# Side-by-side start of a fused two-layer trunk over pieces of weights and activations

## The reference, cut to what matters

```python
h = rms_norm(r, norm_mix_pre[layer])
proj = h @ w_in[layer]          # q latent 384 | kv latent 256 | rope key 32 | dq | dk | dv | gates
# latent attention and differential attention, gated, projected
r = r + rms_norm(mix, norm_mix_post[layer])
h = rms_norm(r, norm_ffn_pre[layer])
r = r + rms_norm((silu(gate) * up) @ w_down[layer], norm_ffn_post[layer])
```

## Time and profile before

| | us |
|---|---|
| median of 3 runs (lowest to highest) | 840.55 (839.25 to 840.62) |
| the profiled execution, its own time | 839.78 |
| its span in the trace | 837.8 |
| PE busy in the span | 820.7 |
| DVE busy in the span | 611.0 |
| ACT busy in the span | 460.1 |
| POOL busy in the span | 127.5 |

### The profile page before, as it was taken

How to read it: one execution, slowest core, us unless ns; L and a number is a source line. 1 busy time by engine, 2 the same in 40 slices (tenths; PEclk the granted TensorE clock), 3 DMA queues, 4 the chain that set the end, 5 groups by cost and what they waited for, 6 DMA issues and landing times.

```text
span 837.8 us, 17756 instructions
## 1 busy us (share of the span) xinstructions
PE 820.7 (98%) x6711; PEld 805.3 (96%) x6711; DVE 611.0 (73%) x1015; ACT 460.1 (55%) x754; POOL 127.5 (15%) x131
## 2 busy tenths in 40 slices
PE   8999999999999999999999999999999999999995
PEld 8998999999999999999999999899999999999995
DVE  5899586569597666666668995866787877667763
ACT  6656555474565444455556556555665744545550
POOL 2112000004331111101112220000143111111010
PEclk9999999999999999999999999999999999999998
DMA  8666423225536555356653665233462665644631
GB/s 289 217 186 203 146 77 101 80 98 190 163 101 217 184 158 186 116 153 183 188 173 107 196 200 178 76 102 101 147 208 75 224 197 182 193 145 150 192 124 51
DMA packets 40554, 131.05 MB, mean 156 GB/s; under 512 B 4528, under 2 KB 5936, under 8 KB 40496
## 3 DMA queue, kind: packets, MB, share of 16 engines
q1 hardware_dynamic: 40496, 130.24, 48.8%
HBM read 129.18 MB, written 1.05 MB: 155 GB/s over the span
## 4 chain that ended last, share of the span: by engine, by line
PE 80%; DVE 14%; ACT 2%; issue 2%; DMA 1%; POOL 0%; SPq 0%; DVEq 0%; POOLq 0%
PE bank L1059 23%; PE bank L1061 22%; PE bank L1060 22%; DVE w_lo L660 4%; PE bank L1089 2%; PE bank L1284 2%; PE bank L1260 2%; PE bank L1108 1%; DVE h_lo L682 1%; PE bank L1299 1%; PE bank L1093 1%; DVE resid L697 1%; DVE tres L690 1%; DVE lat_lo L781 1%; ACT e_t L450 1%
## 5 line engine op out<-in xcount | busy, mean ns | idle before, releaser
L660 DVE TENSOR_TENSOR w_lo<-w_raw,w_hi 128x1024 fp32r<-128x1024 f32 x260 | 347.8, 1344 | 21.7 <-ACT w_hi L321 19.5
L1059 PE MATMUL bank<-h_hi,w_hi 128*128 128x272 f32 (+1 forms) x1232 | 358.3, 291 | 1.9 <-DVE lat L678 0.7
L1061 PE MATMUL bank<-h_hi,w_lo 128*128 128x272 f32 (+1 forms) x1232 | 352.8, 286 | 0.0
L1060 PE MATMUL bank<-h_lo,w_hi 128*128 128x272 f32 (+1 forms) x1232 | 351.8, 286 | 0.0
L321 ACT ACTIVATE w_hi<-w_raw 128x1024 fp32r<-128x1024 f32 x260 | 273.0, 1054 | 117.4 <-PE bank L1061 67.8
L1059 PEld LDWEIGHTS bank<-h_hi,w_hi 128*128 128x128 f32 x1232 | 232.6, 189 | 4.1 <-issue 2.2
L1061 PEld LDWEIGHTS bank<-h_hi,w_lo 128*128 128x128 f32 x1232 | 232.4, 189 | 0.0
L1060 PEld LDWEIGHTS bank<-h_lo,w_hi 128*128 128x128 f32 x1232 | 232.2, 188 | 0.0
L1061 PE MATMUL bank<-ff_hi,w_lo 128*128 128x272 f32 (+1 forms) x352 | 100.0, 284 | 0.0
L1059 PE MATMUL bank<-ff_hi,w_hi 128*128 128x272 f32 (+1 forms) x352 | 99.9, 284 | 0.0
L1060 PE MATMUL bank<-ff_lo,w_hi 128*128 128x272 f32 (+1 forms) x352 | 99.7, 283 | 0.0
(11 more groups left out here) (195 smaller groups left out, 1101.0 us busy)
## 6 DMA issues: line engine op xcount, KB each, us to landing
w_raw<-weights SPq DMA_DIRECT2D x198, 512.0 KB, 3.8
w_raw<-weights SPq DMA_DIRECT2D x32, 384.0 KB, 3.1
w_raw<-weights SPq DMA_DIRECT2D x32, 320.0 KB, 2.8
resid<-x_t SPq DMA_DIRECT2D x4, 272.0 KB, 4.7
out_t<-resid SPq DMA_DIRECT2D x4, 256.0 KB, 2.1
cst<-consts SPq DMA_DIRECT2D x1, 544.0 KB, 5.7
y<-consts SPq DMA_DIRECT2D x1, 256.0 KB, 4.9
b_t<-lam SPq DMA_DIRECT2D x1, 256.0 KB, 5.7
```

The source lines that it names most:

```text
L660: dve.tensor_tensor(w_lo[:, n % RING, :], w_raw[:, n % RAW, :], w_hi[:, n % RING, :].bitcast(f32), ALU.subtract).then_inc(lo_ready, 1)
L1059: pe.matmul(dst, wh, hi, start=first, stop=False)
L1060: pe.matmul(dst, wh, lo, start=False, stop=False)
L1061: return pe.matmul(dst, wl, hi, start=False, stop=last)
```

## The change

The first four slots get an input array of their own, in which each piece is contiguous for each partition, and a buffer of their own (`w_first`, over memory that is used later). The pieces are chunks 0, 1, 2-3, 4-5 and 6-7 of all four slots at once. The activations come in the same pieces; the gains travel in front of the first. Tiles 0 to 3 run side by side, one chunk after another: the high products of a piece first, then those with the low part of the activations, then those with the low part of the weights. Tiles 4 and 5 use banks 4 and 5 and wait for no bank. The norm's sums move from behind tile 2 to behind the first chunk of tile 4, its spread from chunk 6 of tile 3 to chunk 6 of tile 4. The loads of slots 4 to 7 wait for nothing. ScalarE splits slot 6 before the last square instead of after the root. VectorE splits slot 7 at tile 2 together with slot 8, and nothing at tile 1. `keep_clock(50)` becomes `keep_clock(34)`.

```diff
+GAIN_COLS = 80
+FIRST = 4
+PIECES = [(0, 1), (1, 2), (2, 4), (4, 6), (6, 8)]
...
+        (w_first,), _ = place(att0, [("w_first", [P, FIRST * SLOT], f32)])
...
+        def piece_of(w, a, b):
+            return w[:, FIRST * P * a:FIRST * P * b].rearrange("p (s c) -> p s c", s=FIRST)
+        def bank_of(t):
+            return t if t < FIRST + 2 else t % BANKS
...
-                if n >= RAW:
+                if n >= FIRST + RAW:
...
-            sp.dma_start(gain[:, :, :], gains.rearrange("p (l g) -> p l g", l=DEPTH)).then_inc(gain_in, 16)
-            two = weights[0:2 * P, :].rearrange("(s p) c -> p s c", s=2)
-            for q in range(4):
-                sp.dma_start(r[:, 2 * q:2 * q + 2, :], xc[:, 2 * q:2 * q + 2, :]).then_inc(x_in[q], 16)
-                if q in (0, 2):
-                    at = q * SLOT // 4
-                    sp.dma_start(w_raw[:, 0:2, at:at + SLOT // 2], two[:, :, at:at + SLOT // 2]).then_inc(half_in[q // 2], 16)
+            for q, (a, b) in enumerate(PIECES):
+                xs = slice(GAIN_COLS + a * TOK if q else 0, GAIN_COLS + b * TOK)
+                ws = slice(FIRST * P * a, FIRST * P * b)
+                sp.dma_start(x_sb[:, xs], xT[:, xs]).then_inc(x_in[q], 16)
+                sp.dma_start(w_first[:, ws], first_weights[:, ws]).then_inc(piece_in[q], 16)
             sp.dma_start(cst[:, 0:P], consts[:, 0:P]).then_inc(id_in, 16)
-            load(2, SLOT)
-            load(3, SLOT)
             load(4, SLOT)
+            load(5, SLOT)
             sp.dma_start(cst[:, P:], consts[:, 512:C_ALL]).then_inc(tables_in, 16)
-            load(5, SLOT)
+            load(6, SLOT)
+            load(7, SLOT)
...
-            first_hi(0, 1)
-            quarter_split(0)
-            quarter_split(1)
-            first_hi(2, 3)
-            first_squares(0, 1)
-            first_hi(4, 5)
-            quarter_split(2)
-            quarter_split(3)
-            first_hi(6, 7)
-            first_squares(2)
-            split(2)
-            first_squares(3, 4, 5, 6, 7)
-            for n in range(3, AHEAD):
-                split(n)
+            for q in range(len(PIECES)):
+                first_hi(q)
+                piece_split(q)
+                if q >= 2:
+                    first_squares(q - 2)
+            split(FIRST)
+            first_squares(3, 4)
+            split(FIRST + 1)
+            first_squares(5, 6)
+            split(FIRST + 2)
+            first_squares(7)
...
-                if l == 0:
-                    split(AHEAD)
...
+            for q, (a, b) in enumerate(PIECES):
+                dve.wait_ge(x_in[q], 16)
+                for c in range(a, b):
+                    lo_part(0, c, G_MIXPRE, 0, 0)
+                piece_split(q)
+            split(FIRST)
+            split(FIRST + 1)
...
-                    if i or not l:
-                        split(S("lat") + i + AHEAD)
+                    if l or i != 1:
+                        if l == 0 and i == 2:
+                            split(S("lat") + 1 + AHEAD)
+                        if i or not l:
+                            split(S("lat") + i + AHEAD)
...
+            def start_tiles(src):
+                for q, (a, b) in enumerate(PIECES):
+                    for k in range(a, b):
+                        pe.wait_ge(h_hi, k + 1)
...
+                        for t in range(FIRST):
+                            pe.matmul(ps[t][:, :TOK], w_hi[:, t, k * P:(k + 1) * P], src[k][0], start=k == 0, stop=False)
+                    for k in range(a, b):
+                        pe.wait_ge(h_lo, k + 1)
+                        for t in range(FIRST):
+                            pe.matmul(ps[t][:, :TOK], w_hi[:, t, k * P:(k + 1) * P], src[k][1], start=False, stop=False)
...
+                    for k in range(a, b):
+                        for t in range(FIRST):
+                            mm = pe.matmul(ps[t][:, :TOK], w_lo[:, t, k * P:(k + 1) * P], src[k][0], start=False, stop=k == KC - 1)
...
-            keep_clock(50)
+            keep_clock(34)
...
-                    first_tiles([(TL("lat") + q, S("lat") + q, late, t0) for q in range(2)], (h_hi, h_lo, 0),
...
-                    slot_ready(S("lat") + 2)
-                    tile(TL("lat") + 2, S("lat") + 2, 0, P, late, t0)
-                    norm_sums(K0 + PRE_MIX, 7, 0)
-                    pe.wait_ge(id_in, 16)
-                    slot_ready(S("lat") + 3)
-                    tile(TL("lat") + 3, S("lat") + 3, 0, P, full, 0, inside={6: lambda: norm_spread(K0 + PRE_MIX, 7, 0)})
+                    start_tiles(full)
...
+                    tile(TL("lat") + i, S("lat") + i, 0, P if i < 5 else HW, full, 0,
+                         inside={1: lambda: norm_sums(PRE_MIX, 7, 0), 6: first_spread} if (l, i) == (0, 4) else None)
```

More of the change, by code:

```diff
@@ L137, in __init__, with build_trunk @@
                     s += CHUNKS[k]
-def build_trunk(nc: bass.Bass, xT, weights, gains, lam_in, consts, outT):
+def build_trunk(nc: bass.Bass, xT, first_weights, weights, lam_in, consts, outT):
     f32, f32r, bf16 = mybir.dt.float32, mybir.dt.float32r, mybir.dt.bfloat16
@@ L354, in _, with first_hi, piece_split @@
             act.activation(idle_act, eps, ACT.Sqrt)
[L355 to L359, removed]
+            def first_hi(q):
+                act.wait_ge(x_in[q], 16)
+                for c in range(*PIECES[q]):
                     act.activation(hh[:, c, :], r[:, c, :], ACT.Copy, scale=gain[:, 0, G_MIXPRE + c:G_MIXPRE + c + 1]).then_inc(h_hi, 1)
[L362 to L366, removed]
+            def piece_split(q):
+                act.wait_ge(piece_in[q], 16)
+                a, b = PIECES[q]
+                ins = act.activation(w_hi[:, 0:FIRST, a * P:b * P], piece_of(w_first, a, b), ACT.Copy)
+                if b == KC:
+                    ins.then_inc(hi_ready, FIRST)
+                else:
+                    ins.then_inc(piece_hi, 1)
             def first_squares(*chunks):
@@ L677, in evac @@
                 dve.wait_ge(pe_done, plan.tile_done[t])
-                dve.tensor_tensor(dst, ps[t % BANKS][rows, t0:TOK], factor, ALU.mult).then_inc(tile_free, 1)
+                dve.tensor_tensor(dst, ps[bank_of(t)][rows, t0:TOK], factor, ALU.mult).then_inc(tile_free, 1)
             def lo_part(b, c, g, l, t0):
@@ L707, in _, with piece_split @@
             dve.memset(identb[:, :], 0.0).then_inc(warm_ready, 1)
[L708 to L725 removed]
+            dve.wait_ge(x_in[0], 16)
+            def piece_split(q):
+                a, b = PIECES[q]
+                if b == KC:
+                    dve.wait_ge(hi_ready, FIRST)
+                else:
+                    dve.wait_ge(piece_hi, q + 1)
+                ins = dve.tensor_tensor(w_lo[:, 0:FIRST, a * P:b * P], piece_of(w_first, a, b), w_hi[:, 0:FIRST, a * P:b * P].bitcast(f32), ALU.subtract)
+                if b == KC:
+                    ins.then_inc(lo_ready, FIRST)
+                else:
+                    ins.then_inc(piece_lo, 1)
+            for q, (a, b) in enumerate(PIECES):
[5 more added lines that the diff above has]
+            split(FIRST + 1)
             recip(PRE_MIX, 0)
@@ L1172, in _, with first_spread @@
                     slot_ready(S("lat") + i)
-                    tile(TL("lat") + i, S("lat") + i, 0, P if i < 5 else HW, full, 0)
+                    def first_spread():
+                        pe.wait_ge(id_in, 16)
+                        norm_spread(PRE_MIX, 7, 0)
+                    tile(TL("lat") + i, S("lat") + i, 0, P if i < 5 else HW, full, 0,
+                         inside={1: lambda: norm_sums(PRE_MIX, 7, 0), 6: first_spread} if (l, i) == (0, 4) else None)
                 def latent_spreads():
@@ L1487 @@
     gains = np.concatenate(cols, axis=1).transpose(2, 0, 1).reshape(P, DEPTH * GAINS)
+    x_t = np.concatenate([gains, np.zeros((P, GAIN_COLS - DEPTH * GAINS), np.float32), x_t], axis=1)
     lam = np.broadcast_to(A(diff_lambda).reshape(1, DEPTH * 4 * DIFF_DH), (P, DEPTH * 4 * DIFF_DH))
     packed = pack_weights(A(w_in), A(mla_w_uq), A(mla_w_ukv), A(w_o_mla), A(w_o_diff), A(w_out), A(w_gate_up), A(w_down))
-    arrays = {"x_t": x_t, "weights": packed, "gains": gains, "lam": lam, "consts": constants()}
+    first = packed[0:FIRST * P].reshape(FIRST, P, SLOT)
+    first = np.concatenate([first[:, :, a * P:b * P].transpose(1, 0, 2).reshape(P, -1) for a, b in PIECES], axis=1)
+    arrays = {"x_t": x_t, "first_weights": first, "weights": packed, "lam": lam, "consts": constants()}
     arrays = {k: np.ascontiguousarray(v) for k, v in arrays.items()}
```

58 lines of the change are left out of this document (26 added, 32 removed).

## The result

The changed kernel takes 844.89 us in the median of four runs (843.3 to 846.38), against 840.36 for the kernel before (839.25 to 840.62): a ratio of 1.0061, 95% interval 1.0048 to 1.0074 (the two medians alone give 1.0054, inside it). It is slower by 4.5 us by these medians, and 2.8 us above the dearest case that I had priced (842.1). The profiled execution took 844.19, with a span of 842.2, which is 4.4 us more than before.

The account below looks back on a forecast made before the run. VectorE was taken to bound the kernel up to 65 us. Taking the norm's factor 1.3 us sooner, less 0.6 lost at tile 1, gives 0.7: 840.55 - 0.7 = 839.8 us, range 837.9 to 841.5.

Parts of the forecast that it names:

- the dearest case: Clock falls behind the sums inside tile 4 and again at tile 9: 842.1 us.
- VectorE binds from the take to 65 us: From VectorE taking the norm's factor up to 65 us, the schedule hangs on VectorE, not PE.
- the take: VectorE taking the norm's factor, which starts its unbroken work; forecast at 22.3 against 23.64 us, 1.3 us sooner.
- PE starts at 5.0: First weights land at 4.4 us, ScalarE's copy takes 0.58, so PE's real work starts 2.45 us sooner.
- VectorE loses some time at tile 1: With its split moved behind tile 2, VectorE stands about 0.6 us at tile 1, bounds 0 and 0.7.
- PE's lead: PE gains 3.0 + 1.3 us of lead and spends it idle before tiles 6 to 9, mostly ahead of tile 9.
- the sum for the norm: Tile 4's first chunk to 18.4, norm sums to 19.9, five chunks 1.9, spread 0.5: VectorE takes the factor at 22.3 us.
- Chunks 2-3: In the side-by-side tiles, this piece lands at 7.9 us at 338 GB/s, is copied by 8.9; PE waits 0.9 us.
- My slower rival: Clock falls behind the sums inside tile 4: 15 matmuls x 0.10 us, 0.8 us slower, 841.3 us; chance 0.10.
- The line that I drew for the clock: Tile 4's 1.5 us low stretch lies between 1.40 us, where the clock held, and 1.85, where it fell.
- the change gains once all is in time: Factor taken 1.3 us sooner less 0.6 us lost at tile 1 gives 0.7 us net gain at tile 9's start.
- The fit that the prediction took: A transfer costs about 2.0 us fixed plus bytes at 436 GB/s; first weights land near 4.2, PE starts near 4.8.

Follow-up runs that it names:

- early squares: Changed kernel with ScalarE squaring pieces 0 to 2 right behind their high parts and pieces 3 and 4 behind their copies; 841.28 us.
- the other layout: Changed kernel with the first weights stored piece by piece in HBM, rows 2 or 4 KB apart instead of 16; 844.32 us.
- The filled kernel: Changed kernel with 28 warm-up matmuls ahead of the norm sums inside tile 4, in PE's wait for GpSimd's adds; 843.96 us.
- With pairs: Changed kernel with chunks 0 and 1 in one piece, so two chunks per piece throughout, and 50 warm-up matmuls; 842.77 us.
- the split back at tile 1: Changed kernel with VectorE's split put back at tile 1, slot i + 6 at every tile; 843.95 us.
- layout and squares mended: Changed kernel with the first weights stored piece by piece and ScalarE squaring each early piece as soon as it has it; 840.55 us.
- two of its variants: Changed kernel with ScalarE's squares made earlier, 841.28 us, and changed kernel with 28 warm-up matmuls ahead of tile 4's norm sums, 843.96 us.

## Why the prediction was wrong

**Right.** That VectorE binds from the take to 65 us and that the first emptying, which follows the take, decides: the table says so, and between 28 and 72 us VectorE nowhere waits for PE in the changed kernel. That PE starts at 5.0 (4.90; in another execution, with early squares, the first piece came late and it was 6.45). That VectorE loses some time at tile 1 (0.59 us of standing, 0.45 net). That PE's lead is spent waiting ahead of tiles 6 to 9 (3.7 us in three waits, 2.41 of them ahead of tile 9). That root and reciprocal lie beside the five chunks: they run at 23.39 and 23.68, the spread at 26.62.

**The step that failed** is the sum for the norm: "PE does the first chunk of tile 4 to 18.4, the first six sums (0.7 of 1.4 for twelve, rows 3), waits shortly for the last square, ends at 19.9". I asked when the last square would be there and never laid out GpSimd's adds, which stand between each square and the next but one; their chain stood in the sum at nothing. I looked for the bound at the load of slot 6 (its split was over at 20.6 in the profile, and the last square waited for GpSimd, not for it). The terms, in the profile:

- The four tiles and the first chunk ended at 20.2, not 18.4: 1.8 us. Chunks 2-3 began at 10.56, not 8.9; I had 338 GB/s in the start, and it was 208 and 238. This lateness alone would not have set the time: with the other layout PE was there sooner and waited 1.94 instead of 1.65 us for the adds.
- The last add ended at 21.8, so sums from 21.85 to 23.2, which is 3.0 us behind the first chunk and not the 1.5 of my sum: another 1.5 us. The chain of adds begins only at 12.9, since ScalarE squares behind the copies of pieces that come late, and two of its adds take twice their time beside VectorE's subtractions. Early squares alone give back 3.6 us.
- The clock fell behind the sums: 15 x 0.10 = 1.5 us. The filled kernel and the one with early squares show that it holds there when the stretch of waiting and sums is 1.3 us. My slower rival had the place and the price of this fall, and no term for the late adds.

Together 4.8 of the 4.9 us by which the take was missed.

The line that I drew for the clock, held behind 1.40 us and fallen behind 1.85, does not hold up either. With pairs it held behind 2.7 us of waiting and sums, while with the split back at tile 1 it fell after 1.8 us of them and 1.5 us of products. The length of such a stretch alone does not say whether the clock falls, so both my chance for the slower rival and this part of the loss rest on something that the runs do not settle.

Also wrong is that the change gains once all is in time: with layout and squares mended the time is 840.55 against 839.82 (1.0001 to 1.0019), 0.7 us slower instead of faster. The take was then only 0.48 us sooner than before, and the way from the first emptying to tile 9 was 0.44 us longer (16.65 against 16.21); the 0.3 us behind tile 9 are not explained. The change turned PE's wait for weights into a lead for which the next stage had no use, and in doing so put subtractions, squares and adds, which had lain apart, on top of each other.

The Trainium skill ("SBUF — State Buffer", Who interferes with whom) says that a VectorE instruction with two inputs in SBUF contends with a GpSimd instruction that reads SBUF, and calls the pair of ports that they share an exclusive lock. The traces agree that both lose: 1.57 us against 0.78 for an add, and 4.56 us for three subtractions of 816 columns, where 1.21 us for 1024 columns alone would make about 2.9 (an estimate). Read against the diff beforehand, that sentence would have asked where GpSimd adds while VectorE subtracts.

The fit that the prediction took from the Trainium skill ("DMA: Bandwidth & Descriptors", Anatomy of one DMA) is stated there for transfers issued by GpSimd. Here the sync engine issues them; the fit suits the first piece (4.2 against 4.12, where its copy begins) and not piece 2-3 (7.0 by the same working, an estimate, against 9.33).

## What to carry to other kernels

Before moving work forward on the busiest engine, find the one instruction that heads the next stage's unbroken chain (here a copy of 272 columns) and lay out everything that feeds it, side engines too, queue by queue; a lead of the big engine alone was worth nothing here. Helpers that share a resource should be placed by the clock and not where a queue has room. An early start that only shifts the wait also risks the clock behind that wait.

## What the runs showed of the hardware that I had not expected

- GpSimd's add takes up to twice its time beside VectorE's two-input subtractions: 1.57 us instead of 0.78, and four adds 6.04 instead of 4.31 us, when only subtractions were added.
- With pieces of 512 KB throughout, the transfers from 3.5 to 5.0 us ran at 248 to 299 GB/s with rows 16 KB apart and at 395 and 397 with rows 4 KB apart; from 11 to 14 us both ran at over 400 (417 and 420). With chunks 0 and 1 by themselves it was 208 to 282 and 243 to 258, no difference.
- The granted clock fell behind 1.85 us of waiting and sums in the kernel before and behind 3.0 us in the changed one, and held behind 2.7 us with pairs and behind 1.3 us of sums alone. It fell behind waits of 2.2 and 3.2 us for pieces and held behind one of 2.06 us. Behind the same 2.4 us ahead of tile 9 it fell in the changed kernel and held in two of its variants.
- A fall of the clock on an engine that is ahead cost nothing: 12 slow matmuls behind tile 9's wait, and the rest of the span as long as without them (797.8 against 797.7 and 797.8 us).
